# Prompt attention of a hybrid decoder step: rotary queries on GpSimd, an earlier copy of the scaled values, side pieces at other places

## The reference, cut to what matters

```python
q = jnp.einsum('ntq,qhe->nthe', c_q, w_uq)
q_nope, q_pe = q[..., :QK_NOPE], q[..., QK_NOPE:]
q_pe = apply_rope(q_pe, cos[:, None, :], sin[:, None, :])
...
s = (jnp.einsum('qhr,kr->hqk', q_lat, c_kv, preferred_element_type=jnp.float32)
     + jnp.einsum('qhp,kp->hqk', q_pe, k_pe, preferred_element_type=jnp.float32)) * SOFTMAX_SCALE
s = jnp.where(k_pos[None, None, :] <= q_pos[None, :, None], s, NEG_INF)
p = jax.nn.softmax(s, axis=-1)
o = jnp.einsum('hqk,kr->qhr', p.astype(rows.dtype), c_kv, preferred_element_type=jnp.float32)
...
o = jnp.einsum('nthr,rhv->nthv', o_lat, w_uv)
return o.reshape(n, t, N_HEADS * V_HEAD) @ w_o
```

## Time and profile before

| what | value |
|---|---|
| median of three runs | 2622.91 us |
| profiled execution | 2613.51 us |
| its span, first to last instruction | 2611.7 us |
| TensorE busy over the span | 2470.5 us (95%) |
| VectorE, ScalarE, GpSimd busy | 1091.3, 559.3, 600.3 us |
| mean granted TensorE clock | 0.983 |
| prompt attention in the trace | about 1090 to 1590 us |

### The profile page before, as it was taken

How to read it: one execution, slowest core, us unless ns; L and a number is a source line. 1 busy time by engine, 2 the same in 40 slices (tenths; PEclk the granted TensorE clock), 3 DMA queues, 4 the chain that set the end, 5 groups by cost and what they waited for, 6 DMA issues and landing times.

```text
span 2611.7 us, 35877 instructions
## 1 busy us (share of the span) xinstructions
PE 2470.5 (95%) x13347; PEld 2117.0 (81%) x13347; DVE 1091.3 (42%) x1975; ACT 559.3 (21%) x961; POOL 600.3 (23%) x364
## 2 busy tenths in 40 slices
PE   8899999999999979989898999988999999999996
PEld 8799999999999767576666675448999999999995
DVE  4343344334443642334444445432444344433446
ACT  3311111111111342332222222433111101111112
POOL 2422222222222420000000000232222222222225
PEclk9999999999999989999999999998999999999998
DMA  5101110111101111000000002231101111011111
GB/s 171 57 25 48 48 48 25 48 48 48 45 28 48 45 47 47 9 9 17 17 17 17 9 9 77 81 125 57 49 26 46 48 48 46 26 48 48 48 32 69
DMA packets 132443, 117.84 MB, mean 45 GB/s; under 512 B 8896, under 2 KB 119448, under 8 KB 132352
## 3 DMA queue, kind: packets, MB, share of 16 engines
q1 hardware_dynamic: 132368, 116.83, 14.4%
HBM read 110.94 MB, written 6.42 MB: 45 GB/s over the span
## 4 chain that ended last, share of the span: by engine, by line
PE 91%; DVE 4%; ACT 2%; issue 2%; POOL 0%; DMA 0%; SPq 0%; ACTq 0%; DVEq 0%
PE ps L643 21%; PE ps L642 21%; PE ps L644 21%; PE ps L922 4%; PE ps L988 3%; PE ps L892 2%; PE ps L975 1%; PE ps L864 1%; PE ps L1072 1%; PE ps L906 1%; PE ps L897 1%; PE ps L712 1%; PE ps L1047 1%; PE ps L938 1%; PE ps L1031 1%
## 5 line engine op out<-in xcount | busy, mean ns | idle before, releaser
L642 PE MATMUL ps<-XH,WGH 128*128 128x368 f32 x2112 | 699.8, 331 | 18.0 <-POOL WGL L1813 13.5
L643 PE MATMUL ps<-XL,WGH 128*128 128x368 f32 x2112 | 699.9, 331 | 0.0
L644 PE MATMUL ps<-XH,WGL 128*128 128x368 f32 x2112 | 697.3, 330 | 0.0
L1561 DVE TENSOR_TENSOR XR<-XR,ps 128x512 f32<-128x512 f32 x756 | 510.6, 686 | 8.4 <-PE ps L644 4.5
L1544 DVE TENSOR_TENSOR HF<-SG,ps 128x368 f32<-128x368 f32 x132 | 71.0, 538 | 940.1 <-PE ps L644 934.3
L642 PEld LDWEIGHTS ps<-XH,WGH 128*128 128x128 f32 x2112 | 398.6, 189 | 22.6 <-issue 19.2
L643 PEld LDWEIGHTS ps<-XL,WGH 128*128 128x128 f32 x2112 | 398.1, 189 | 1.9
L644 PEld LDWEIGHTS ps<-XH,WGL 128*128 128x128 f32 x2112 | 398.3, 189 | 0.0
L1804 POOL TENSOR_TENSOR HL<-HF,HH 128x368 fp32r<-128x368 f32 x132 | 129.7, 983 | 853.1 <-DVE HH L1548 853.1
L642 PE MATMUL ps<-WDH,HH 128*128 128x512 f32 (+1 forms) x792 | 311.7, 394 | 5.6 <-DVE XR L1561 5.6
L644 PE MATMUL ps<-WDH,HL 128*128 128x512 f32 (+1 forms) x792 | 314.3, 397 | 0.0
(11 more groups left out here) (208 smaller groups left out, 2801.1 us busy)
## 6 DMA issues: line engine op xcount, KB each, us to landing
RAWG<-ffn_w_gate SPq DMA_DIRECT2D x44, 512.0 KB, 5.6
RAWG<-ffn_w_up SPq DMA_DIRECT2D x44, 512.0 KB, 6.8
RAWD<-ffn_w_down SPq DMA_DIRECT2D x44, 512.0 KB, 3.4
CR<-cache_mla_l SPq DMA_DIRECT2D x64, 160.0 KB, 2.6
XR<-x_prompt SPq DMA_DIRECT2D x8, 512.0 KB, 12.7
WOP<-mla_w_o SPq DMA_DIRECT2D x8, 512.0 KB, 3.3
WOA<-mla_w_o SPq DMA_DIRECT2D x1, 4096.0 KB, 17.4
o_y_prompt<-XR SPq DMA_DIRECT2D x8, 512.0 KB, 2.6
```

Source lines behind the costliest of these rows:

```text
L642: pe.matmul(out, w[0], x[0], start=start, stop=False)
L643: pe.matmul(out, w[0], x[1], start=False, stop=False)
L644: return pe.matmul(out, w[1], x[0], start=False, stop=stop)
L1561: dve.tensor_tensor(XR[0:r, t, ds], XR[0:r, t, ds], ps[0:r, 4 + 2 * w + half, :], ALU.add).then_inc(s_row[2 * l + 1], 1)
```

## The change

The rotary copies and the remainder move from ScalarE and VectorE to GpSimd, which does the two copies behind its memsets of steps 2 and 4 and the remainder behind that of step 6, and for head 0 before its first memsets. ScalarE copies ORW of a unit within that unit, between its second and its third group of pieces. The counts of pieces per group are new for the first head, odd heads and even heads; the last head keeps its own. The order of the pieces and the rule for banks stay.

```diff
-SHARE = ([(1, 1, 0)] * 5 + [(0, 1, 0)] + [(0, 0, 0)] * 3, [(1, 1, 1)] * 9, [(0, 0, 0)] + [(0, 1, 1)] * 8)
+SHARE_FIRST = [(1, 1, 0)] * 4 + [(0, 1, 0)] * 3 + [(0, 0, 0)] * 2
+SHARE_ODD = [(0, 1, 1), (0, 2, 1), (1, 1, 1), (0, 1, 1), (0, 2, 2), (1, 2, 1), (1, 2, 1), (1, 1, 1), (0, 1, 1)]
+SHARE_EVEN = [(0, 2, 1)] + [(1, 1, 1)] * 8
+SHARE_LAST = [(0, 0, 0)] + [(0, 1, 1)] * 8
+ROPE_AFTER = (2, 4, 6)
...
-            share = SHARE[0 if h_ == 0 else 2 if h_ == H - 1 else 1]
+            share = (SHARE_FIRST if h_ == 0 else SHARE_LAST if h_ == H - 1 else SHARE_ODD if h_ % 2 else SHARE_EVEN)
...
-            rope_queries(0)
             for f in range(len(projection(0))):
                 side_act(f)
             act.wait_ge(h_init, 3)
             exponentials(0)
             for u in range(NU):
-                h = UNITS[u][0]
                 for f in PLAN[u][0]:
                     side_act(f)
-                if u >= 1:
-                    output_rows(u - 1)
                 if u + 1 < NU:
                     exponentials(u + 1)
                 for x, g in enumerate(chunks(UNITS[u][1])):
                     k = GROUP_AT[u] + x
                     if k % 2 == 0:
                         evacuate_probabilities(act, copy, u, k, g).then_inc(h_ta, 1)
-                for part in PLAN[u][1:]:
-                    for f in part:
-                        side_act(f)
-                if u % NQ == 2 and h + 1 < H:
-                    rope_queries(h + 1)
-            output_rows(NU - 1)
+                for f in PLAN[u][1]:
+                    side_act(f)
+                output_rows(u)
+                for f in PLAN[u][2]:
+                    side_act(f)
...
-            rope_queries_low(0)
             dve.wait_ge(h_init, 3)
...
-                if u % NQ == 2 and h + 1 < H:
-                    rope_queries_low(h + 1)
...
+            def rope_queries(h, half):
+
+                if h >= 2:
+                    pool.wait_ge(h_s, NQ * (h - 1))
+                at = ROPE * (h % 2)
+                pool.wait_ge(h_qh, 2 * h + half)
+                pool.tensor_copy(QRS[ROPE * half:ROPE * half + ROPE, h % 2, :], QPT[at:at + ROPE, h // 2, :]
+                                 ).then_inc(h_qh, 1)
+
+            def rope_queries_low(h):
+                at = ROPE * (h % 2)
+                pool.wait_ge(h_qh, 2 * (h + 1))
+                pool.tensor_tensor(QRS[at:at + ROPE, h % 2, :], QPT[at:at + ROPE, h // 2, :],
+                                   QRS[at:at + ROPE, h % 2, :].bitcast(F32), ALU.subtract).then_inc(h_ql, 1)
+
+            pool.wait_ge(q_ev, NT)
+            rope_queries(0, 0)
+            rope_queries(0, 1)
+            rope_queries_low(0)
+            pool.wait_ge(h_ql, 1)
             pool.wait_ge(h_fill, 1)
             pool.memset(PR[:], 0.0).then_inc(h_init, 1)
...
                 pool.memset(PR[:, u % 2, n:(n + P - 1) // P * P], 0.0).then_inc(h_z, 1)
+                h, step = UNITS[u][0] + 1, u % NQ
+                if h < H and step in ROPE_AFTER[:2]:
+                    pool.wait_ge(h_z, u + 1)
+                    rope_queries(h, ROPE_AFTER.index(step))
+                    pool.wait_ge(h_qh, 2 * h + ROPE_AFTER.index(step) + 1)
+                if h < H and step == ROPE_AFTER[2]:
+                    pool.wait_ge(h_z, u + 1)
+                    rope_queries_low(h)
+                    pool.wait_ge(h_ql, h + 1)
```

More of the change, by code:

```diff
@@ L1306, in _ @@
             act.wait_ge(q_ev, NT)
[L1308 to L1315, removed]
             def side_act(f):
@@ L1640, in _ @@
             dve.tensor_tensor(KRL[:], MT[:, 6, 0:KEYS], KRH[:].bitcast(F32), ALU.subtract).then_inc(h_kr, 1)
[L1642 to L1646, removed]
             def side_dve(f):
```

## The result

The changed kernel took 2571.59 us (median of 4 runs, 2571.08 to 2572.72); the kernel before, beside it, 2617.64 (4 runs, 2612.14 to 2624.51). The ratio is 0.9828, with a 95% interval of 0.9802 to 0.9853: 46 us less by the medians, and 42.4 by the profiled executions (2613.51 and 2571.08). The runs of the kernel before fall into two groups, near 2613 and near 2623 us, and the profiled one is of the lower group, which is why the two differences differ.

A forecast was written before the change was run, and what follows sets the result against it. TensorE bounds the prompt attention, standing still 43.9 of 500 us. Savings per head plus 1.1 us of clock sum to 44.4 us: 2613.5 becomes 2569, put at 2574 us for run scatter; range 2563 to 2597.

The forecast's parts named there:

- the new waits: TensorE in odd heads: 0.5 us for WKT and 0.18 for three output pieces in a row, 0.68 per head.
- The restart: TensorE: each wait costs its idle time plus 0.26 us for the drained pipeline, added for every wait that goes.
- Order and rope: Prompt attention: earlier ORW copy and rotary work on GpSimd remove ORW waits, including 2.7 us standstills; 25 us with clock.
- The pieces: New counts per group remove TensorE's waits for banks (QTL, VT, XR) in odd and even heads.
- The 15 pairs: Two pieces in a second group, costed at 0; rival 1 said same-bank waits cost 15.6 us, chance 0.10.
- nothing moved to other steps: Rival 2: bank waits are moved, not removed, so only 25 us is won, 2588 or 2593 us; chance 0.10.
- The new WKT wait: First value piece waits for transposed WKT, copied by ScalarE behind an exponential; between 0 and 0.7+0.26 us, taken as 0.5.
- The 0.18 for the row of three output pieces: At step 4 to 5, the third piece comes 1.72 us after the first; a bank is free after 1.90.
- GpSimd: Two copies at 1.8 us and a 2.6 us subtraction per head, 6.2 us, hidden; cost 0, also at the start.
- the cover: GpSimd's memset is due two units later, so TensorE would notice only from about 14 us per operation.
- Rival 3: GpSimd's 24 new operations block VectorE's small two-SBUF-input ones and hold banks: 59 us cost, 2628 us, slower; chance 0.05.
- The clock: After the last 2.7 us standstill TensorE's clock is low; removing the standstill wins at least 1.1 us.

The follow-up runs named there:

- the part kernels: Kernels with one edit each in the kernel before, or one undone in the changed kernel; stages 497.09 to 523.41 us, against 531.05 before and 487.98 after.
- the kernel without the pieces: Changed kernel with the old counts of pieces per group: stage 508.46 us against 487.98 changed and 531.05 before; 2592.30 us in all.
- the order alone: Kernel before with only ScalarE's ORW copy moved ahead of the last pieces: stage 523.41 us, 7.6 less; median 2609.34 us over ten runs, ratio 0.9968.
- the rope alone: Kernel before with only the rotary copies and remainder moved to GpSimd: stage 517.85 us, 13.2 less; 2598.54 us in all.
- the kernel without the rope: Changed kernel with rotary copies on ScalarE and remainder on VectorE again: stage 505.88 us, 17.9 more than changed; 2594.39 us in all.
- eight copies: Changed kernel with each rotary copy done eight times on GpSimd from head 1 on: stage 488.06 us against 487.98; 2572.76 us in all.
- 20 transposes: Changed kernel with 20 more ORW transposes on TensorE at the attention's end: stage 1.74 us longer, total 8.95 us longer, 2580.54 us.

## Why the prediction was right

**What bounds it.** TensorE's standstill was the thing to win, and its waits by head named nearly all of it. Added up over the stage, the named waits fell from 43.3 us to 8.4, by 34.9; the terms of the sum had 35.8 less the 2.0 of the new waits. TensorE's idle time in the attention, forecast near 8 us, was 9.8.

**The restart.** I added 0.26 us to each wait that goes. The 35 waits fewer would give 9.1 us. Measured: 43.1, less 34.9 of waits, less 1.7 of clock, leaves 6.5 us, 0.19 each. The addition was right, but 40% too large; without it the sum would have been 35 us. Over the part kernels the same remainder is 0.1 to 0.34, so it is no constant. That a drained pipeline is its cause, as I wrote, no run shows; they show the time.

**Order and rope.** The 25 us of these two (with the clock) were 22.6 in the kernel without the pieces. What is missing is a term that I put at nothing: where ORW's waits of the odd heads go, waits for QTL and WKT come out from behind them, 2.8 us in all. The new counts of pieces take these away too, so the sum of all parts didn't suffer; that the parts' errors met in this way I had not foreseen. "That wait is counted above and goes only if both edits work" was half right: the order alone takes nothing from a 2.7 us standstill, the rope alone all but 0.3. I named ScalarE's copies in front of that wait, and "VectorE loses the subtraction and its wait for the copies" without a price. The order alone shows that VectorE's wait is 2.7 us of TensorE by itself, and the kernel without the rope that it is 9.5 us of waits and 8.4 of clock.

**The pieces.** 44.4-25 = 19.4 us by the sum; 18.95 alone, in part by luck (ORW waits that went, a clock that fell), and 20.5 on top of order and rope, 2.8 of them the waits that the order had brought out. The 15 pairs cost nothing; nothing moved to other steps. The new WKT wait was 0.2 us, near the lower end of 0 to 0.96, not 0.5; it shows in two of the three odd heads. The 0.18 for the row of three output pieces doesn't show at all.

**GpSimd.** The copy was mis-sized: 1.10 us where I took 1.8 between 0.97 and 2.63. The subtraction, at 2.54, was 2.6. Minimum, median and maximum in ns:

```profile
L1834 POOL CAST QRS<-QPT x16: 1096/1102/1107, 1071.0 to 1462.1; 64x1104 fp32r<-64x1104 f32 x16
L1840 POOL TENSOR_TENSOR QRS<-QPT,QRS x8: 2517/2542/3380, 1073.3 to 1474.9; 64x1104 fp32r<-64x1104 f32 x8
```

A one-input copy is near the memset, not in the middle. Nothing depended on it, since the cover holds to at least 9.3 us. At the start VectorE began its first low part at 1079.36, 8.88 us after QPT; before it was 1080.93-1072.11 = 8.82: no cost, as said.

**Rival 3.** The lock is there. The one subtraction of 3.38 us ran beside VectorE's subtraction with two SBUF inputs:

```profile
1073.07 1.27 DVE L1630 TENSOR_TENSOR KRL<-MT,KRH 128x1040 fp32r<-128x1040 f32 x1 [3.18 <-ACT KRH L1151]
1073.33 3.38 POOL L1840 TENSOR_TENSOR QRS<-QPT,QRS 64x1104 fp32r<-64x1104 f32 x1
```

The Trainium skill (SBUF — State Buffer, Who interferes with whom) says that one of the two waits for the whole instruction of the other; the trace agrees: 3.38-2.54 = 0.84 us more for GpSimd, which started 1.01 us before VectorE ended. Which of the two waits changed with who started first: in three of the other kernels (the rope alone, eight copies, 20 transposes) GpSimd's subtraction started 0.26 us before VectorE's and took 2.50 to 2.51 us, and VectorE's took 3.35 to 3.36 in place of 1.27. What the rival got wrong is how often they meet, and that a late sum would hold TensorE back. In the changed kernel none of VectorE's 24 small operations was hit (153 and 160 ns at most); with eight copies one was, and the stage was not longer.

**The clock, and the total.** Of the low clock in the stage I took 1.1 us; it was 1.7, the upper end that I had named. The clock of the later stretch wasn't in the sum: it took 2.3 us back, and the earlier start of the stage gave 1.6, which is scatter (it starts between 1071.1 and 1073.95 us in these kernels). The sum said 2569 beside the profile, which measured 2571.1; the forecast of 2574 lies 2.4 us above the measured median.

## What to carry to other kernels

Before an engine's wait is priced, follow the other engines' lists at that moment: a standstill with two causes stays when one of them is removed, the named releaser is only the last, and a wait that goes can bring out another that stood hidden behind it. Compare a change by the stage that it touches, from one marker instruction to another, because an unchanged later stage, here of 1006.4 to 1017.0 us, can add or hide some 10 us by its clock. When a part's time agrees with its forecast, compare its waits too: here one agreed because two unforeseen terms cancelled. Give an engine with room the work, but count how long its own next duty may be late: here 9.3 us cost nothing, and 23.3 us, fourteen times, cost 112 us in all.

## What was not expected of the hardware

Three standstills of 2.7 us that look alike were followed by a granted clock of 0.50 after one, two or three of them, depending on the kernel; where all three were, it cost 6.8 us in one kernel and 8.4 in another, by estimate. A stage of unchanged instructions was granted 0.91, 0.89 or 0.83 over 120 us, and 1.74 us more ahead of it went with 7.7 us more in and after it. A GpSimd copy of 64x1104 from float32 took 1.10 us, 1.0 ns a column, and its two-input subtraction 2.54 us.
